# Decoder step: rotary on feature-major heads in place of row-major heads, and a seventh buffer set for expert weights

## The chip, the cores and the metric

The kernel runs on one core of a Trainium2 chip, in float32. The metric is the device time of one launch in microseconds (us), taken as the median of several runs. All other times below are from one profiled execution.

## The reference

One layer of a decoder trunk, for a prompt of 256 tokens and a sample group of 8 tokens (each with 1024 cached positions), 264 tokens in all.

```python
h = rmsnorm(x)
rq, rk, rv, rg, aq, ak, av, gr, ga = split(h @ w_in)        # 8192 columns, 64 groups of 128
rq, aq = rope(rq, pos) * 128**-0.5, rope(aq, pos) * 128**-0.5
rk, ak = rope(rk, pos), rope(ak, pos)                       # x1*cos - x2*sin, x2*cos + x1*sin
r = retention(rq, rk, rv, state)     # 4 heads, chunks of 128; group norm; silu(rg)
a = attention(aq, ak, av, cache)     # 8 heads; the sample group reads 64 cached pages of K and of V
x = x + (sigmoid(gr) * (r @ w_ret_o) + sigmoid(ga) * (a @ w_att_o)) @ w_o
x = x + hier_moe(rmsnorm(x))         # 32 experts (1024 -> 256 -> 1024), two per token
y = rmsnorm(x)                       # outputs: y, the rotated ak, av, the retention states
```

## The kernel before

Every engine runs a program written out by hand, and semaphores tie them together; inside one engine (and inside one DMA-issuing queue) the order is that of the code. A projection unit is 128 output features for all 264 tokens: `features` multiplies 8 weight blocks into `zps[m % 2]` with features on partitions and tokens along the row. Units m = 0 to 63 are the input projection: 0 to 7 the attention queries (one head each), 8 to 15 the keys, 16 to 23 the values, 24 to 27 the retention queries, 28 to 31 the retention keys, 32 to 39 the retention values, 40 to 47 the retention gate, 48 to 63 the two sigmoid gates. Units 64 to 71 multiply by `w_ret_o`, 72 to 79 by `w_att_o`, 80 to 87 by `w_o`. The weights of the units come through a ring of six 1 MB slots (`ring_all`), two units in each.

For m below 40 ScalarE copies `zps` to `zt[m % 2]`, and one unit later TensorE transposes `zt` into rows (three transposes: two blocks of 128 tokens, and 8 sample tokens) in `nps`, which ScalarE copies to `zatt` or `zret` (prompt) and `zdec` or `dret` (sample). GpSimd (`turn`) then rotates the query and key rows in place, two heads at a time with six products or sums: 128x256 each for the prompt, 8x128 each for the sample. TensorE turns rotated heads back to features on partitions where a score needs them: `a_stage(h, 0)` (4 transposes for attention head h, at unit 24 + 3h), `r_stage(r, 0)` (4 for retention head r, at unit 40 + 4r), and `sample_turn` (8 small ones at unit 42). ScalarE copies each result to `qkT`, `rqkT` or `qkd`.

VectorE works at the same time on the sample group's 64 cached key pages (`page`: eight products of 128x128 with a sum, one for each head, L1402). `pages_by(m)` says how many of them stand ahead of unit m in its program: 14 by unit 23, then 7 in four units up to unit 40. Between them stand the softmax steps of the prompt (`a_max` at unit 25 + 3h, `a_scale` after the page behind it), retention (`r_mask`, `r_norm`, `r_gate`) and, from unit 49 on, the sample states. ScalarE waits for `a_max` in its program at unit 25 + 3h, ahead of the `zt` copy of the next unit; TensorE's unit m + 2 waits for that copy. At units 49 to 60 each of the 8 sample states goes through a chain: `gain<-v_rows` from GpSimd's queue, VectorE, TensorE, and out again.

After the projections TensorE multiplies 64 cached value pages (L1087), does `w_ret_o`, `w_att_o` and `w_o`, and the tokens are routed. In the expert stage the tokens of a pair of experts are gathered from `h2_rows` into `xg`, transposed (`x_tr`, L1201), multiplied by gate and up weights (`gate_up`, L1212) and by the down weights, four experts at a time (`quad_down`, L1235). An expert's weights are 3 MB in three 1 MB loads; `SETS` = 6 sets of buffers hold them, placed over buffers that earlier stages no longer need. Loads of experts 0 to 5 stand in SyncE's program ahead of the expert stage; the loads of gate and up of expert e behind them wait for `e_GU` to reach e + 1 - SETS, those of down for `e_D`.

Of the kernel before, what the change touches and what calls it, by code (L numbers as in the profile page):

```python
# [47 lines left out]
SETS = 6  # L48
# [17 lines left out]
def shape_constants():  # L66
# [18 lines left out]
    rope = np.zeros((P, 3, 4, 64), np.float32)  # L85
    for t in range(3):
        pos = i + P * t if t < 2 else np.full(P, PAST, np.float32)
        ang = (pos[:, None].astype(np.float32) * inv[None, :]).astype(np.float32)
        rope[:, t, 0], rope[:, t, 1] = np.cos(ang), np.sin(ang)
        rope[:, t, 2], rope[:, t, 3] = np.cos(ang) * DH ** -0.5, np.sin(ang) * DH ** -0.5  # L90
    put("rope", rope.reshape(P, -1))
# [72 lines left out]
N_ROWS = 40  # L164
# [4 lines left out]
def build(nc, x_prompt, x_sample, cache_k, cache_v, state_ret, page_table, norm_mix, w_in, w_ret_o, w_att_o,  # L169
# [3 lines left out]
    with ctx:  # L173
# [6 lines left out]
        def sem(name):  # L180
# [17 lines left out]
        lgs = sb("lgs", [G + NE, T])  # L198
# [9 lines left out]
        zt = [sb(f"zt{i}", [P, T]) for i in range(2)]  # L208
        qb_all = sb("qb", [P, 2, DM])
# [34 lines left out]

        pw = zr[:, 1984:1984 + NPG * 512 + 64]
# [18 lines left out]
        xgT = [zflat[:, 3 * DM + 512 * i:3 * DM + 512 * (i + 1)] for i in range(2)]  # L264
# [5 lines left out]
        h2n = zflat[:, 0:3 * DM].rearrange("p (t d) -> p t d", t=3)  # L270
# [63 lines left out]
        a_T, a_Tc, a_S, a_P, a_PT, a_PTc, a_O, a_Oc, a_mx, a_ex = map(sem, (  # L334
# [35 lines left out]
        def _(sp):  # L370
# [143 lines left out]
        def _(pool):  # L514
# [114 lines left out]
            for p in range(2):  # L629
                gather_for(p)  # L630
# [1211 lines left out]
```

## Time and profile before

| | |
|---|---|
| median of 3 runs | 761.89 us (760.59 to 765.05) |
| the profiled execution | 762.18 us, of which 760.4 us are the span from first to last instruction |
| busy, share of the span | TensorE 86%, VectorE 40%, ScalarE 19%, GpSimd 18% |
| moved | 243 MB, 320 GB/s over the span |

A busy share is an average over stages with different limits, so the stages are read apart below. The chain of waits is followed back from the last instruction, at each step to what released it; the table of waits says what an engine stood still for. "PEclk" is the clock that was granted to TensorE, as a share of 2.4 GHz.

### The profile page before, as it was taken

To read this page: it belongs to the slowest core of one execution; us is meant where nothing else is said; L and a number is where in the kernel's file an instruction comes from. 1 tells how busy PE (TensorE), PEld (TensorE's weight loads), DVE (VectorE), ACT (ScalarE), POOL (GpSimd) and SP (SyncE) were. 2 spreads that over 40 slices of the span, in tenths; PEclk is the share of its full clock that TensorE was granted. 3 is DMA by queue.
4 is the path that set the end of the run, shared out by engine and by line. 5 is a ranking of instruction groups with operands and counts; after the bars stand their busy time and mean duration, and the time that the engine had idled before them with its cause. 6 is when DMAs were issued, how large, how long until landed. Compare 5 with 4: busy or idle time off the path is not lost.

```text
span 760.4 us, 13782 instructions
## 1 busy us (share of the span) xinstructions
PE 655.6 (86%) x5037; PEld 461.6 (61%) x5037; DVE 306.8 (40%) x1552; ACT 142.4 (19%) x406; POOL 139.0 (18%) x209
## 2 busy tenths in 40 slices
PE   5999999998999978999998999927897879667674
PEld 3888888677888856755432877626653445434331
DVE  3004987998868588610000121354324111111103
ACT  3122223233325322120010000120100101101013
POOL 0169964762000223200000000011000000000000
PEclk9999999999999999999999999957999898899997
DMA  9938989889988988977999989366999999999971
GB/s 309 260 127 281 312 271 401 288 279 342 360 292 281 392 273 287 382 275 275 390 409 386 297 320 409 140 256 239 361 394 401 348 382 401 402 400 402 416 285 59
DMA packets 94918, 243.00 MB, mean 320 GB/s; under 512 B 8850, under 2 KB 54546, under 8 KB 86530
## 3 DMA queue, kind: packets, MB, share of 16 engines
q1 hardware_dynamic: 57906, 192.99, 67.7%
q10 hardware_dynamic: 31328, 32.00, 12.7%
q0 software_dynamic: 5616, 17.11, 6.8%
q8 instruction: 42, 0.69, 0.4%
q14 instruction: 26, 0.21, 0.1%
HBM read 235.00 MB, written 9.11 MB: 321 GB/s over the span
## 4 chain that ended last, share of the span: by engine, by line
PE 56%; DMA 25%; DVE 13%; SPq 2%; issue 2%; ACT 1%; ACTq 0%; POOL 0%; DVEq 0%; POOLq 0%
PE zps L913 32%; DVE kall L1402 6%; PE nps L1087 5%; DMA ring_all<-in_w_up 5%; PE nps L1212 4%; DMA kall<-in_w_up 3%; DMA zret<-in_w_up 3%; DMA gain<-v_rows 3%; DMA qb<-in_w_down 3%; DMA ring_all<-in_w_ret_o 3%; PE zps L1235 3%; DMA out<-sfin 2%; PE nps L884 2%; DMA ring_all<-in_w_down 1%; SPq L444 1%
## 5 line engine op out<-in xcount | busy, mean ns | idle before, releaser
L913 PE MATMUL zps<-hT,ring_all 128*128 128x264 f32 x1152 | 274.8, 393 | 1.6 <-DVE hT L1583 1.0
L913 PEld LDWEIGHTS zps<-hT,ring_all 128*128 128x128 f32 x1152 | 217.4, 193 | 45.0 <-issue 5.3
L1402 DVE CUSTOM_DVE_ANT_0 kall<-kall,qb 128x128 f32<-128x128 f32 x512 | 153.0, 364 | 60.0 <-DMA kall<-in_cache_k 56.9
L620 POOL DMA_INDIRECT zatt<-h_rows,tidx_i x16 | 15.0, 939 | 349.4 <-DVEq L1671 194.4
L913 PE MATMUL zps<-headT,ring_all 128*128 128x264 f32 x256 | 58.5, 388 | 3.7 <-DMA ring_all<-in_w_ret_o 2.3
L913 PEld LDWEIGHTS zps<-headT,ring_all 128*128 128x128 f32 x256 | 48.1, 190 | 14.8 <-issue 4.8
L1087 PE MATMUL nps<-ring_all,zret 128*64 128x512 f32 x224 | 51.6, 599 | 2.8 <-DMA ring_all<-in_cache_v 2.8
L1745 DVE TENSOR_TENSOR qdT<-qdT,nps 128x64 f32<-128x64 f32 x32 | 7.1, 221 | 107.5 <-ACT qdT L825 107.0
L669 ACT ACTIVATE zt<-zps 128x264 f32<-128x264 f32 x56 | 21.8, 390 | 149.4 <-PE zps L913 148.0
L1212 PE MATMUL nps<-ring_all,zatt 128*32 128x128 f32 x768 | 30.0, 311 | 13.9 <-DMA ring_all<-in_w_up 12.4
L1570 DVE TENSOR_TENSOR hT<-zps,zatt 128x264 f32<-128x264 f32 x8 | 3.5, 433 | 93.1 <-PE zps L913 92.9
L1402 DVE DVE_READ_ACCUMULATOR2_ANT scores<- 128x1 f32 x512 | 40.4, 79 | 0.0
L1212 PEld LDWEIGHTS nps<-ring_all,zatt 128*32 128x32 f32 x768 | 25.4, 125 | 17.8 <-issue 16.4
L1761 DVE TENSOR_TENSOR xs<-xs,zps 8x512 f32<-8x512 f32 x15 | 10.1, 675 | 64.3 <-PE zps L1254 64.3
L825 ACT ACTIVATE qdT<-nps 128x64 f32<-128x64 f32 x32 | 7.2, 224 | 144.9 <-PE nps L1212 144.9
L1087 PEld LDWEIGHTS nps<-ring_all,zret 128*64 128x64 f32 x224 | 14.7, 136 | 31.5 <-issue 23.3
L884 PE MATMUL nps<-cst,zt 128*128 128x128 f32 x128 | 22.1, 275 | 3.7 <-ACT zt L669 3.6
L1235 PE MATMUL zps<-zatt,scores 128*32 128x512 f32 x40 | 21.0, 651 | 3.7 <-DMA qb<-in_w_down 3.7
L602 POOL DMA_DIRECT2D gain<-v_rows x16 | 8.8, 549 | 82.7 <-DVE xs L1485 77.7
L1223 PEld LDWEIGHTS nps<-cst,qdT 64*64 64x64 f32 x128 | 6.7, 133 | 28.0 <-issue 27.5
L1235 PE MATMUL zps<-ring_all,scores 128*32 128x512 f32 x88 | 22.4, 630 | 0.7 <-DMA hT<-in_w_down 0.7
L1201 PE MATMUL zps<-cst,zatt 64*128 64x64 f32 x128 | 17.6, 283 | 5.2 <-DMA zatt<-h_rows,tidx_i 5.2
(364 smaller groups left out, 839.5 us busy)
## 6 DMA issues: line engine op xcount, KB each, us to landing
kall<-in_cache_k SPq DMA_DIRECT2D x64, 512.0 KB, 6.4
ring_all<-in_cache_v SPq DMA_DIRECT2D x56, 512.0 KB, 8.2
ring_all<-in_w_in ACTq DMA_DIRECT2D x26, 1024.0 KB, 8.8
ring_all<-in_w_gate SPq DMA_DIRECT2D x12, 1024.0 KB, 15.6
ring_all<-in_w_up SPq DMA_DIRECT2D x12, 1024.0 KB, 17.6
ring_all<-in_w_down SPq DMA_DIRECT2D x10, 1024.0 KB, 15.7
ring_all<-in_w_in SPq DMA_DIRECT2D x6, 1024.0 KB, 13.6
kall<-in_w_gate SPq DMA_DIRECT2D x5, 1024.0 KB, 22.8
```

Of the source, the lines that this page charges most:

```text
L444: sp.dma_start(gate_up_w[b][:, a, :], w[0, bass.ds(e, 1)].rearrange("o (p k) f -> p (o k f)", k=KT)).then_inc(gu_in[b], 16)
L602: pool.dma_start(vb[c], v_rows[b:b + 1, 512 * c:512 * (c + 1)].partition_broadcast(P) .rearrange("p o d -> p (o d)")).then_inc(vb_in[c], 16)
L620: pool.indirect_dma_start(out=rows, out_offset=None, in_=h2_rows, in_offset=bass.IndirectOffsetOnAxis(ap=col, axis=0), bounds_check=T - 1, ...
L669: return act.activation(out, in_, ACT.Copy)
L884: return pe.transpose(out, in_, ident[0:rows, 0:rows])
L913: mm = pe.matmul(zps[m % 2][:, 0:T], w[:, k, P * fb:P * (fb + 1)], rhs[:, k, :], start=(k == 0), stop=(k == KT - 1))
L1087: mm = pe.matmul(nps[0][64 * c:64 * (c + 1), :], pw[:, 512 * p + 64 * b:512 * p + 64 * (b + 1)], pages[:, DM * k + 512 * c:DM * k + 512 * ...
L1201: mm = pe.transpose(zps[0][:, 2 * CAP * k:2 * CAP * k + rows], xg[par][0:rows, k:DM:KT], ident[0:rows, 0:rows])
L1212: mm = pe.matmul(nps[par][CAP * q:CAP * (q + 1), 0:P].rearrange("p (a f) -> p a f", a=2), x[:, 2 * CAP * k:2 * CAP * k + CAP], w[:, :, k, ...
L1235: mm = pe.matmul(bank[CAP * i:CAP * (i + 1), 0:512], acT[q % 2][:, 64 * i + CAP * f:64 * i + CAP * (f + 1)], down_w[b].rearrange("p (f n) ...
L1402: ins = v.tensor_tensor_reduce(kh, kh, qb[b % 2][:, P * h:P * (h + 1)], 1.0, 0.0, ALU.mult, ALU.add, scores[:, pg, AH * b + h:AH * b + h + 1])
L1761: v.tensor_tensor(at, at, bank[0:NB, :], ALU.add).then_inc(e_Sc, 1)
```

## The change

Queries and keys (units 0 to 15 and 24 to 31, `ROTATED`) are rotated as they come out of the projection, with features on partitions. ScalarE makes three copies (`own_copy`): `zps` to `zt`, and its two halves exchanged to `zs`, with the query scale in the copy. GpSimd (`rotate`) multiplies `zt` by cosines, `zs` by signed sines, and adds, each 128x264, into a buffer of the head's own (`turned`). The scores read these buffers, so `a_stage(h, 0)`, `r_stage(r, 0)` and `sample_turn` are gone, with their copies. Rows are made two units after the projection and only for what an output or a row-wise step needs: sample rows alone for attention queries, all for attention keys, none for retention queries, prompt rows for retention keys, which ScalarE scales by the decay on the way to `kdd`. Buffers move to make room: `gain`, `rows_a`, `rows_b` take over work of `zatt` in the expert stage, and `norm_final` is loaded at the end by SyncE. A seventh set of expert weights lies in `zatt` and in `cst`. The gathered rows of odd pairs lie on partitions 64 to 127, and `x_tr` uses a plain product with the identity in place of a transpose.

```diff
-SETS = 6
+SETS = 7
+M_ROWS = 40
+ROTATED = [*range(16), *range(24, 32)]
+ROW_JOBS = [*range(24), *range(28, M_ROWS)]
+def row_jobs(m):
+    return [(j, q) for j, q in enumerate(ROW_JOBS) if q + (2 if q in ROTATED else 1) == m]
...
+            gate_up_in(6, 6)
             sp.wait_ge(z_ready, 2 * (N_IN + 2 * N_O))
             gate_up_in(5, 5)
...
             down_in(1, 1)
+            down_in(6, 6)
...
+            sp.wait_ge(e_GU, NE)
+            sp.dma_start(gain[:, :], norm_final.rearrange("(o d) -> o d", o=1).partition_broadcast(P)
...
-            def turn(x, tmp, tab, rows, nt, q):
-                pool.tensor_tensor(ta, x2, sin, ALU.mult)
-                link(pool.tensor_tensor(tb, x1, sin, ALU.mult))
-                pool.tensor_tensor(x1, x1, cos, ALU.mult)
-                link(pool.tensor_tensor(x2, x2, cos, ALU.mult))
-                pool.tensor_tensor(x1, x1, ta, ALU.subtract)
-                link(pool.tensor_tensor(x2, x2, tb, ALU.add))
+            def rotate(i):
+                m = ROTATED[i]
+                a, _ = COL["rope"]
+                pool.wait_ge(zt_done, m + 1)
+                pool.tensor_tensor(zt[m % 2][:, :], zt[m % 2][:, :], cst[:, a:a + T], ALU.mult)
+                link(pool.tensor_tensor(zs[m % 2], zs[m % 2], cst[:, a + T:a + 2 * T], ALU.mult))
+                pool.tensor_tensor(turned[i], zt[m % 2][:, :], zs[m % 2], ALU.add).then_inc(rope_done, 1)
...
+            def own_copy(m):
+                if m >= 2:
+                    if m - 2 in ROTATED:
+                        act.wait_ge(rope_done, ROTATED.index(m - 2) + 1)
+                    else:
+                        act.wait_ge(n_ready, ROW_JOBS.index(m - 2) + 1)
+                z, ps = zt[m % 2], zps[m % 2]
+                if m in ROTATED:
+                    scale = DH ** -0.5 if m < 8 or 24 <= m < 28 else 1.0
+                    act.activation(z[:, :], ps[:, 0:T], ACT.Copy, scale=scale)
+                    act.activation(zs[m % 2][0:64, :], ps[64:128, 0:T], ACT.Copy, scale=scale)
+                    act.activation(zs[m % 2][64:128, :], ps[0:64, 0:T], ACT.Copy, scale=scale).then_inc(zt_done, 1)
...
-                if k == 0:
-                    pe.wait_ge(rope_done, 8)
-                    for a in range(2):
-                        for t in range(2):
-                            mm = tr(mps[:, 256 * a + P * t:256 * a + P * (t + 1)],
-                                    zatt[:, t, 1024 * a + P * h:1024 * a + P * (h + 1)], P)
-                    mm.then_inc(a_T, 1)
                 if k == 1:
-                    pe.wait_ge(a_Tc, h + 1)
+                    pe.wait_ge(rope_done, 16)
-                    pe.matmul(mps[:, 512:640], qkT[:, 0:128], qkT[:, 256:384], start=True, stop=True)
+                    pe.matmul(mps[:, 512:640], qT[h][:, 0:128], kT[h][:, 0:128], start=True, stop=True)
...
-                    mm = pe.transpose(zps[0][:, 2 * CAP * k:2 * CAP * k + rows], xg[par][0:rows, k:DM:KT], ident[0:rows, 0:rows])
+                    mm = pe.matmul(zps[0][:, 2 * CAP * k:2 * CAP * k + rows], xg[par][0:rows, k:DM:KT], ident[at, at],
+                                   start=True, stop=True, tile_position=(2 * CAP * par, 0))
```

TensorE at units 25 to 27, before (L913 is a projection unit, L884 and L925 make rows or turn heads, L953 and L954 are the scores):

```order
L884 MATMUL nps<-cst,zt 128x128 x2
L925 MATMUL nps<-cst,zt 8x128
L953 MATMUL mps<-scr 128x128
L954 MATMUL mps<-scr 128x256
L913 MATMUL zps<-hT,ring_all 128x264 x8
L884 MATMUL nps<-cst,zt 128x128 x2
L925 MATMUL nps<-cst,zt 8x128
L913 MATMUL zps<-hT,ring_all 128x264 x8
L884 MATMUL nps<-cst,zt 128x128 x2
L925 MATMUL nps<-cst,zt 8x128
L884 MATMUL mps<-cst,sm 128x128 x3
L884 MATMUL mps<-cst,zatt 128x128 x4
```

and in the changed kernel (L903 is the projection unit, L874 a transpose, L952 and L953 the scores):

```order
L903 MATMUL zps<-hT,ring_all 128x264 x8
L952 MATMUL mps<-headT 128x128
L953 MATMUL mps<-headT 128x256
L903 MATMUL zps<-hT,ring_all 128x264 x16
L874 MATMUL mps<-cst,sm 128x128 x3
L903 MATMUL zps<-hT,ring_all 128x264 x8
L952 MATMUL mps<-headT 128x128
L953 MATMUL mps<-headT 128x256
L945 MATMUL mps<-pT,zatt 128x128
L946 MATMUL mps<-pT,zatt 128x128
L947 MATMUL mps<-pT,zatt 128x128
```

The row transposes of the retention queries (`nps<-cst,zt`) and the four transposes of the next head (`mps<-cst,zatt`) are gone from between the units; the scores read `headT`.

GpSimd around the outputs of values, before: two of the output issues, the prompt part of two retention heads, the start of their sample part:

```order
L567 DMA out<-zatt 128x1024 x2
L569 DMA out<-zdec 8x1024
L530 TENSOR_TENSOR rtmp<-zret,cst 128x4x64
L531 TENSOR_TENSOR rtmp<-zret,cst 128x4x64
L532 TENSOR_TENSOR zret<-zret,cst 128x2x2x64
L533 TENSOR_TENSOR zret<-zret,cst 128x2x2x64
L534 TENSOR_TENSOR zret<-zret,rtmp 128x2x2x64
L535 TENSOR_TENSOR zret<-zret,rtmp 128x2x2x64
L530 TENSOR_TENSOR rtmd<-zdec,cst 8x2x64
L531 TENSOR_TENSOR rtmd<-zdec,cst 8x2x64
L532 TENSOR_TENSOR zdec<-zdec,cst 8x2x64
L533 TENSOR_TENSOR zdec<-zdec,cst 8x2x64
```

and in the changed kernel, heads 24 and 25 ahead of all output issues, and head 26 behind them:

```order
L542 TENSOR_TENSOR zt<-zt,cst 128x264
L543 TENSOR_TENSOR zret<-zret,cst 128x264
L544 TENSOR_TENSOR zatt<-zt,zret 128x264
L554 DMA out<-zatt 128x1024 x2
L556 DMA out<-zdec 8x1024
L559 DMA out<-zatt 128x1024 x2
L561 DMA out<-zdec 8x1024
L542 TENSOR_TENSOR zt<-zt,cst 128x264
L543 TENSOR_TENSOR zret<-zret,cst 128x264
L544 TENSOR_TENSOR zatt<-zt,zret 128x264
```

Three 128x264 operations for a head stand where there were six of 128x256 and six of 8x128 for two.

SyncE's queue ahead of the expert stage, before:

```order
L448 DMA ring_all<-in_w_down 128x2x1024 [waits z_ready]
L444 DMA headT<-in_w_gate 128x2048 [waits z_ready]
L444 DMA headT<-in_w_up 128x2048
L444 DMA ring_all<-in_w_gate 128x2048 [waits z_ready]
L444 DMA ring_all<-in_w_up 128x2048
L448 DMA ring_all<-in_w_down 128x2x1024 [waits z_ready]
L448 DMA hT<-in_w_down 128x2x1024 [waits z_ready]
L448 DMA scr<-in_w_down 128x2x1024 [waits logits_T]
L448 DMA qb<-in_w_down 128x2x1024 [waits h2_root]
```

and in the changed kernel:

```order
L456 DMA ring_all<-in_w_down 128x2x1024 [waits z_ready]
L452 DMA zatt<-in_w_gate 128x2048
L452 DMA zatt<-in_w_up 128x2048
L452 DMA headT<-in_w_gate 128x2048 [waits z_ready]
L452 DMA headT<-in_w_up 128x2048
L452 DMA ring_all<-in_w_gate 128x2048 [waits z_ready]
L452 DMA ring_all<-in_w_up 128x2048
L456 DMA ring_all<-in_w_down 128x2x1024 [waits z_ready]
L456 DMA cst<-in_w_down 128x2x1024
L456 DMA hT<-in_w_down 128x2x1024 [waits z_ready]
L456 DMA scr<-in_w_down 128x2x1024 [waits logits_T]
L456 DMA qb<-in_w_down 128x2x1024 [waits h2_root]
```

Gate and up of expert 6 (into `zatt`) now stand ahead of those of expert 5, and its down weights (into `cst`) behind those of expert 1.

## Rows read from the trace of the kernel before

**Rows 1.** The page: TensorE's busy time, and the DMA busy share in 40 slices

```profile
PE 655.6 (86%) x5037; PEld 461.6 (61%) x5037; DVE 306.8 (40%) x1552; ACT 142.4 (19%) x406; POOL 139.0 (18%) x209
...
DMA  9938989889988988977999989366999999999971
```

**Rows 2.** Windows by stage: us, busy us of each engine, PEclk, DMA share, GB/s

```profile
26.50:116.50 90.00, 90.00 (x444) 76.36 (x442) 44.92 (x219) 21.31 (x79) 61.92 (x100) 1.00 0.75 251
116.50:202.90 86.40, 82.39 (x416) 65.35 (x415) 78.00 (x483) 28.22 (x85) 38.55 (x58) 0.98 0.94 334
202.90:248.30 45.40, 45.40 (x244) 39.66 (x243) 35.17 (x256) 19.73 (x46) 1.11 (x2) 1.00 0.84 291
248.30:320.50 72.20, 63.17 (x321) 48.22 (x320) 49.83 (x279) 17.03 (x49) 21.09 (x28) 0.95 0.93 329
320.50:420.00 99.50, 92.91 (x427) 45.02 (x425) 7.62 (x20) 8.26 (x23) 0.00 (x0) 1.00 0.93 349
420.00:492.00 72.00, 70.00 (x321) 55.62 (x320) 15.65 (x45) 4.89 (x12) 0.00 (x0) 1.00 0.78 292
492.00:516.00 24.00, 7.31 (x83) 5.74 (x82) 12.53 (x59) 5.32 (x6) 1.98 (x2) 0.59 0.62 231
516.00:741.00 225.00, 176.60 (x2704) 109.77 (x2704) 48.71 (x158) 25.01 (x87) 13.05 (x14) 0.91 0.97 374
```

**Rows 3.** Chain of waits, 14 to 130 us: start, us, what, count

```profile
26.46 0.33 PE nps L884 x3
...
26.79 3.56 PE zps L913 x16
...
116.26 0.44 PE mps L884 x4
...
120.26 0.22 PE nps L884 x2
...
120.48 0.31 PE nps L925 x2
```

**Rows 4.** TensorE's waits, 14 to 315 us: total, times, longest

```profile
PE nps L1017 <- DVE headT L1468: 4.8, 1, 4.8
...
PE nps L884 <- ACT zt L669: 3.6, 2, 1.9
```

**Rows 5.** Timeline around 130 us: start, us, engine, line, operation

```profile
126.42 0.29 DVE L1402 CUSTOM_DVE_ANT_0 kall<-kall,qb 128x128 f32<-128x128 f32 x1
...
126.54 0.76 POOL L530 TENSOR_TENSOR rtmp<-zret,cst 128x256 f32<-128x256 f32 x1 [7.83 <-ACT zdec L669]
...
126.64 0.81 DVE L1402 CUSTOM_DVE_ANT_0 kall<-kall,qb 128x128 f32<-128x128 f32 x1
...
131.47 0.59 POOL L530 TENSOR_TENSOR rtmd<-zdec,cst 8x128 f32<-8x128 f32 x1
...
134.88 0.28 DVE L1402 CUSTOM_DVE_ANT_0 kall<-kall,qb 128x128 f32<-128x128 f32 x1
```

**Rows 6.** Chain of waits over the whole span

```profile
247.63 17.48 DMA out<-sfin
```

**Rows 7.** Windows ahead of and in the expert stage

```profile
470.00:490.00 20.00, 20.00 (x92) 14.96 (x91) 4.77 (x14) 3.33 (x8) 0.00 (x0) 1.00 0.53 208
505.00:520.00 15.00, 7.54 (x131) 6.22 (x131) 2.70 (x10) 0.03 (x1) 2.91 (x3) 0.50 0.21 67
620.00:680.00 60.00, 45.34 (x649) 27.35 (x638) 9.28 (x20) 6.32 (x22) 3.17 (x4) 0.89 1.02 397
```

**Rows 8.** Timeline of SyncE's queue, first expert load inside the expert stage

```profile
519.97 0.34 SPq L444 DMA_DIRECT2D ring_all<-in_w_gate  x1
```

**Rows 9.** Timeline of TensorE, the first pair's transposes

```profile
514.30 1.11 PE L1201 MATMUL zps<-cst,zatt 64*128 64x64 f32 x8 [5.18 <-DMA zatt<-h_rows,tidx_i]
```

**Rows 10.** Timeline of the tail

```profile
732.43 0.22 ACT L825 ACTIVATE qdT<-nps 128x64 f32<-128x64 f32 x1 [4.28 <-PE nps L1212]
...
748.87 1.21 DVE L1806 TENSOR_TENSOR ring_all<-xs,gain 8x1024 f32<-8x1024 f32 x1 [0.54 <-DVE xs L1761]
```

More of the change, by code:

```diff
@@ L55 @@
 _WIDTHS = [("ident", P), ("ones", P), ("upper", P), ("causal", 3 * P), ("rmask", RH * P), ("rdec", RH * P),
-           ("kdec", RH), ("rope", 3 * 4 * 64), ("edge", EDGES), ("slot", CAP), ("order", NE),
-           ("val", 6), ("tile", XT), ("diag", NB * NB), ("own", AH),
-           ("before", 16), ("after", 16), ("spread", NB * AH)]
+           ("kdec", RH), ("rope", 2 * T), ("diag", NB * NB), ("own", AH), ("spread", NB * AH), ("edge", EDGES), ("slot", CAP),
+           ("order", NE), ("val", 6), ("tile", XT), ("before", 16), ("after", 16)]
 COL, _at = {}, 0
@@ L84, in shape_constants @@
     inv = (np.float32(10000.0) ** (-np.arange(64, dtype=np.float32) / np.float32(64))).astype(np.float32)
[L85 to L91, printed above, removed]
+    pos = np.concatenate([np.arange(S), np.full(NB, PAST)]).astype(np.float32)
+    ang = (pos[None, :] * np.concatenate([inv, inv])[:, None]).astype(np.float32)
+    sign = np.where(i < 64, -1, 1)[:, None]
+    put("rope", np.concatenate([np.cos(ang), sign * np.sin(ang)], 1))
     put("edge", np.tile(CAP * np.arange(1, EDGES + 1) - 0.5, (P, 1)))
@@ L242, in build @@
         vo = zr[:, 0:512]
+        part = lambda ap, at, n: [ap[:, at + T * k:at + T * (k + 1)] for k in range(n)]
+        qT = part(headT[:, 0, :], 0, AH)
+        kT = part(headT[:, 1, :], 0, 5) + part(zflat, 0, 3)
+        rqT = part(scr, 1024, 1) + part(zflat, 3072, 3)
+        rkT = part(zr, 0, 3) + part(zr, 3072, 1)
+        zs = part(zr, 3072 + T, 2)
+        turned = qT + kT + rqT + rkT
         pw = zr[:, 1984:1984 + NPG * 512 + 64]
@@ L263, in build @@
             down_w[i] = ring[(g + 2) % RING]
-        xgT = [zflat[:, 3 * DM + 512 * i:3 * DM + 512 * (i + 1)] for i in range(2)]
+        xgT = [gain[:, 512 * i:512 * (i + 1)] for i in range(2)]
         acT = [scores_f[:, 256 * i:256 * (i + 1)] for i in range(2)]
@@ L622, in gather @@
                                         bounds_check=T - 1, oob_is_err=False).then_inc(x_in2[par], 16)
-            def gather_for(p):
+            for p in range(NPAIR):
                 if p >= 2:
@@ L627, in gather_for @@
                 gather(p % 2, xg[p % 2], tidx_i[0:2 * CAP, p:p + 1])
-            for p in range(2):
-                gather_for(p)
-            for p in range(2, NPAIR):
-                gather_for(p)
             base = link_n[0]
@@ L788, in _ @@
             load_x()
-            act.dma_start(gain[:, :], norm_final.rearrange("(o d) -> o d", o=1).partition_broadcast(P)
-                          .rearrange("p o d -> p (o d)")).then_inc(fgain, 16)
             for k in range(KT):
```

251 lines of the change are left out of this document (105 added, 146 removed).

## Prediction

> **What bounds the kernel now.** I read the page first, then windows by stage, then the chain of waits inside the stages that the change touches. On the page TensorE is busy for 86% of the span and the DMA engines are seldom below 80% [rows 1], so two limits are close everywhere, and the stage decides which one counts. From 26.5 to 116.5 us TensorE never pauses (90.0 of 90.0 us) and the DMA share is 0.75: TensorE is the bound. From 116.5 to 202.9 it is busy for 82.4 of 86.4 us, VectorE for 78.0, and the DMA share is 0.94: three near-bounds. From 202.9 to 248.3 TensorE is full again. From 248.3 to 320.5 it pauses 9 us while the sample states go round. The value stage (320.5 to 420) has 0.93 of DMA beside 92.9 of 99.5 us of TensorE; the next stage is TensorE's, with a DMA share of 0.78; routing (492 to 516) is a chain of small steps, with TensorE at half its clock or little more; and the experts (516 to 741) run at a DMA share of 0.97 with TensorE idle for 48 us: DMA bound [rows 2].
>
> In the chain of waits a projection unit is 3.56 us of products and 0.33 us for three row transposes, 0.11 us each. Turning a head back for the scores is 0.44 us. In the units whose sample rows go to partition 32, rows cost 0.22 us for two transposes and about 0.31 us for the plain product [rows 3]; I round this to 0.63 us a unit for all and 0.31 us for the product.
>
> The 4 us of pauses from 116.5 to 202.9 come from VectorE. In its table of waits 3.6 us, in two pieces, are for ScalarE's `zt` copy [rows 4]; that copy stands behind ScalarE's wait for `a_max`. VectorE is late because of GpSimd. One product of a key page takes 0.29 us alone, and follows the one before by 0.22 us; beside a GpSimd operation it takes 0.81 us. Between 126.64 and 131.47 GpSimd ran six operations of 128x256 and VectorE got eight products through, which alone take 1.7 us of those 4.8: 0.52 us of VectorE lost per operation. From 131.47 to 134.88 six operations of 8x128 let nine products through, 1.9 us of 3.4: 0.25 us lost per operation, however few partitions it has [rows 5].
>
> **The change, part by part.**
>
> Projection, units 2 to 24. Rows of attention queries need one transpose where they needed three: 8 units x 0.22 = 1.8 us. The first head's 0.44 us goes too. TensorE is full here, so all 2.2 us count. ScalarE makes three copies for one, but drops row copies; it is busy for 21 us of these 90 [rows 2], which covers the added 0.3 us each. A new loop appears: the copy of unit m waits for the rotation of m - 2. It costs some 1 us of copies and three GpSimd operations of 0.77 to 0.82 us, 3.5 us in all, against two units of more than 3.6 us each: covered twice. GpSimd alone needs 2.5 us a unit and is covered as well.
>
> Units 25 to 40 (116.5 to 202.9 us). Removed from TensorE: 5 heads x 0.44, retention head 0 at 0.44, the rows of four retention queries at 0.63, and the sample product of four retention keys at 0.31: 6.4 us. The pauses are the second part. From here on VectorE loses to GpSimd, before, 24 operations x 0.52 + 24 x 0.25 + 2.1 us beside two decay products of 128x512 (taken as four of 128x256), 20.6 us; after, 8 heads x 3 x 0.52 = 12.5 us. Its own demand in this stage, 29 key pages x 8 x 0.21 and six softmax steps that I put at 2 us, is 61 us. That makes 82 us before, as much as TensorE was busy, so that each lateness of VectorE became a pause; and 74 us after, beside 82.4 - 6.4 = 76 us of TensorE. With all pauses gone the stage gives 10.4 us. I take 9.5, because the DMA share of 0.94 leaves little: the same 28.9 MB (334 GB/s x 86.4 us) in 76.9 us is 376 GB/s. Bounds: 5.2 us if the DMA time of 0.94 x 86.4 can't be compressed at all, 12 us if the half-clock units after a pause go as well.
>
> The Trainium skill weighs in on both halves of this. "SBUF — State Buffer", section "Who interferes with whom", says that a VectorE operation with two SBUF inputs and a GpSimd operation that reads SBUF exclude each other for a whole instruction. By that as a loss of GpSimd's full 0.8 and 0.55 us the demand before would be 61 + 35 = 96 us, more than the stage took; the trace shows turns being taken, and the loss is the measured 0.52 and 0.25 us. "HBM Reference", section "Specifications (TRN2)", gives 358 GB/s as a core's share of a domain, with more for a core that streams alone; by 358 this stage could not go below 80.7 us and would give 5.7.
>
> Units 41 to 48: two attention heads and two retention heads at 0.44 us and eight transposes of 8 rows (below the 0.9 us of eight full ones; I take 0.6), 2.4 us, of which I count 2.3, TensorE full [rows 2].
>
> Units 49 to 63: the fourth retention head's 0.44 us lies beside pauses of 9 us. One is TensorE's 4.8 us behind VectorE [rows 4], which comes from a 17.5 us write of a 128 KB retention state that `r_norm` waits for [rows 6]. Nothing of that is touched. 0 us; bounds: 5 us either way, since that write may fall into a quieter or a busier moment.
>
> Value stage: 0.5 MB of `norm_final` leaves it, 1.5 us at 349 GB/s [rows 2], half hidden: 0.5 us (0 to 1.5). At the end the same load is issued once the last gate-and-up product is done, 732 us, and is needed at 748.9 us [rows 10]: it costs nothing as long as it lands in 16 us.
>
> Experts. Each load set is 3 MB, 3.15 million bytes, at the 397 GB/s of the steady part [rows 7] 7.9 us. Loads inside the stage start at 520 us [rows 8] and from there DMA bounds it; with seven sets 25 experts are loaded there and not 26. The extra 3 MB needs time ahead of the stage, and there is some: the DMA share is 0.53 from 470 to 490 and 0.21 from 505 to 520 us [rows 7], 21 us idle. Gain 7.9 us; bounds: 0 if the extra loads push experts 5 and 0 to 4 late, 8.4 us at the stage's mean of 374 GB/s.
>
> Its price: `x_tr` becomes eight plain float32 products, each two instructions. The eight transposes take 1.11 us [rows 9]; sixteen instructions at 0.11 to 0.155 us [rows 3] take 1.7 to 2.5 us. The first pair lies on the path to the first `e_GU`, so I add 0.9 us (0 to 1.4). The other 15 lie in TensorE's 48 idle us [rows 2].
>
> Sum: -2.2 - 9.5 - 2.3 - 0.5 - 7.9 + 0.9 = -21.5. The profiled execution took 762.18 us, 0.3 us from the median of the runs, so the sum gives 740.7: **741 us**.
>
> **The rivals.**
>
> A: the front's gain is given back. For it: DMA shares of 0.94 and 0.93 [rows 2], and the sample states' chain, which runs at DMA latency. Against it: TensorE never waits for a projection weight there. If units 25 to 40 give 4 us and the state chain takes 3 us more, the sum is -21.5 + 5.5 + 3 = -13: 749 us.
>
> B: the seventh set gives nothing, because something before 520 us comes late or the queue's `e_D` waits leave gaps. For it: SyncE's queue is in order, and one gap shows in the windows' 0.97. Against it: the same waits come at the same counts. -21.5 + 7.9 = -13.6: 748.5 us.
>
> C: more than forecast: all pauses of units 25 to 40 go and the 17.5 us write with its 4.8 us wait does not recur: -21.5 - 2.5 - 4.8, 733 us.
>
> D: slower: the rotation becomes the pace of 24 units. It decides once a GpSimd operation costs over 1.2 us (3 x 1.2 = 3.6 us, a unit); at 1.6 us it adds 24 x (4.8 - 3.6) = 29 us, and the kernel ends at 741 + 29 = 770 us. Against it: 0.76 us measured for nearly the same shape [rows 5].
>
> **How the numbers follow.** The likeliest case (734 to 747 us by its terms' bounds) has 0.53, A 0.18, B 0.10, C 0.12, D 0.05, and 0.02 is left for something else. A measurement of this kernel tells about 0.5% from no change, 3.8 us. Faster: all but D and a little of A, 0.92; same 0.03; slower 0.05. The range takes in C and A with B: 732 to 753 us.
>
> **What would show it.** In the profile after: the first 24 units in steps of 3.67 us while queries are rotated, and no pauses; units 25 to 40 in 75 to 79 us, with VectorE's mean for L1402's product below 0.33 us from 0.36; GpSimd's three operations at 0.75 to 0.9 us; the stretch of units 49 to 63 still some 70 us; the step from the start of the experts' first product to the last down product about 217 us where it was 225, at 0.97 DMA or more. The prediction is wrong if key pages wait for their DMA for more than 5 us in units 25 to 40 (A), if the expert stage keeps its 225 us (B), or if TensorE waits for ScalarE's copy in units 2 to 24 (D).

## The result, and the profile after

The changed kernel took **768.71 us** in the median of 4 runs (767.35 to 770.15), the kernel before 761.5 us beside it (4 runs): ratio 1.0085, 95% interval 1.0053 to 1.0118. It is slower by 0.9%. I had forecast 741 us, in a range of 732 to 753: the time is outside the range, and the sign is wrong. The profiled execution spans 768.3 us. A run more than 1.5% above the fastest of its kernel is left out of every median and ratio; that is one run in all, in experiment 4.

The page of the changed kernel, first the lines that answer to [rows 1], then two groups of TensorE (matmul and weight load: count | busy us, mean ns | idle before):

```profile
PE 694.2 (90%) x5069; PEld 501.4 (65%) x5069; DVE 282.8 (37%) x1552; ACT 149.0 (19%) x425; POOL 100.9 (13%) x136
...
DMA  9948998899989689879999698837599969999981
...
L1176 PE MATMUL zps<-cst,rows_b 64*128 64x64 f32 x256 | 64.6, 407 | 5.1 <-DMA rows_b<-h_rows,tidx_i 5.1
L1176 PEld LDWEIGHTS zps<-cst,rows_b 64*128 64x128 f32 x256 | 62.1, 331 | 8.5 <-issue 8.5
```

GpSimd and VectorE lost work, as was meant (139.0 to 100.9 us, 306.8 to 282.8). TensorE, which was to lose some 11 us in the front and gain 10 to 22 in the experts, went from 655.6 to 694.2. One line holds it: `x_tr`'s products take 64.6 us.

The windows by stage, cut at the starts of units 25, 41, 49 and 64 and at the experts' first transposition; columns as in [rows 2]. First the kernel after, then the kernel before at the same places:

```profile
113.07:192.92 79.85, 74.94 (x367) 61.64 (x366) 65.78 (x443) 28.48 (x88) 25.52 (x35) 0.96 0.92 326
192.92:230.69 37.77, 37.77 (x192) 32.84 (x191) 32.63 (x237) 13.44 (x31) 1.28 (x3) 1.00 0.91 312
230.69:316.37 85.68, 71.69 (x364) 55.52 (x363) 57.50 (x322) 20.80 (x60) 21.04 (x28) 0.94 0.89 322
505.80:748.90 243.10, 229.99 (x2840) 159.70 (x2840) 49.35 (x158) 24.84 (x87) 13.08 (x14) 0.88 0.87 335
```

```profile
116.53:202.88 86.35, 82.34 (x415) 65.30 (x414) 77.95 (x483) 28.19 (x85) 38.55 (x58) 0.98 0.94 334
202.88:243.19 40.31, 40.31 (x216) 35.14 (x215) 31.16 (x225) 16.65 (x38) 1.11 (x2) 1.00 0.81 278
243.19:324.89 81.70, 72.29 (x368) 55.94 (x366) 57.25 (x320) 21.06 (x60) 21.09 (x28) 0.96 0.94 338
514.30:741.10 226.80, 177.71 (x2712) 110.69 (x2712) 49.19 (x158) 25.01 (x87) 13.05 (x14) 0.90 0.96 371
```

The first column after the window is its length. Units 25 to 40 went from 86.4 to 79.9 us, units 41 to 48 from 40.3 to 37.8, units 49 to 63 from 81.7 to 85.7; the experts' stage from 226.8 to 243.1. It starts 8.5 us earlier than before and ends 7.8 us later. In it TensorE has only 13 idle us of 243, where it had 49 of 227, and the DMA share fell from 0.96 to 0.87. The bound has changed hands: the stage that was the DMA engines' is now TensorE's.

The waits say the same. TensorE's in the expert stage (total us, times, longest), after and then before:

```profile
PE nps L1199 <- DVE qdT L1721: 6.4, 9, 0.8
PE zps L1176 <- DMA rows_b<-h_rows,tidx_i: 5.1, 1, 5.1
PE nps L1211 <- DMA hT<-in_w_down: 3.1, 1, 3.1
PE nps L1188 <- DMA kall<-in_w_up: 1.3, 1, 1.3
```

```profile
PE nps L1212 <- DMA ring_all<-in_w_up: 12.4, 4, 4.3
PE nps L1223 <- DVE qdT L1745: 12.2, 12, 3.4
...
PE nps L1212 <- DMA headT<-in_w_up: 4.9, 2, 4.3
PE nps L1212 <- DMA zdec<-in_w_up: 4.3, 1, 4.3
PE zps L1235 <- DMA qb<-in_w_down: 3.7, 2, 3.2
PE nps L1212 <- DMA kall<-in_w_up: 3.2, 1, 3.2
PE nps L1212 <- DMA zret<-in_w_up: 2.8, 2, 1.7
PE nps L1235 <- DMA ring_all<-in_w_down: 2.2, 1, 2.2
...
PE zps L1235 <- DMA hT<-in_w_down: 0.7, 1, 0.7
```

Before, TensorE waited for expert weights fourteen times, 34.2 us in all; now twice, 4.4 us. The other side of it stands in SyncE's queue, which issues those loads once TensorE has used the buffer: its waits for gate-and-up products grew from 38.1 to 56.7 us, for down products from 76.6 to 99.6.

What one pair costs can be read from TensorE's timeline. After, in the middle of the stage:

```profile
600.79 4.07 PE L1176 MATMUL zps<-cst,rows_b 64*128 64x64 f32 x16
604.78 0.48 PE L1199 MATMUL nps<-cst,qdT 64*64 64x64 f32 x4
605.19 3.64 PE L1188 MATMUL nps<-zatt,gain 128*32 128x128 f32 x64
```

Before, the same three steps:

```profile
519.84 1.09 PE L1201 MATMUL zps<-cst,zatt 64*128 64x64 f32 x8
520.86 0.33 PE L1223 MATMUL nps<-cst,qdT 64*64 64x64 f32 x4
521.12 1.95 PE L1212 MATMUL nps<-ring_all,zatt 128*32 128x128 f32 x64
```

The pair takes 4.07 us where I had put 1.7 to 2.5, and the gate-and-up product right behind it takes 3.64 instead of 1.95 us: it runs at half the clock, and nothing idle stands ahead of it.

### The profile page after: what moved, and what is told of

The parts are those of the page before. It is cut to its first block, busy times and chain, and to the rows that moved or that the text cites. A ratio compares the mean times of both kernels' runs of the same rounds, so it can differ in the third digit from the quotient of the medians.

```text
span 768.3 us, 13775 instructions
## 1 busy us (share of the span) xinstructions
PE 694.2 (90%) x5069; PEld 501.4 (65%) x5069; DVE 282.8 (37%) x1552; ACT 149.0 (19%) x425; POOL 100.9 (13%) x136
## 4 chain that ended last, share of the span: by engine, by line
PE 73%; DMA 15%; DVE 7%; ACT 2%; issue 2%; SPq 1%; ACTq 0%; DVEq 0%; POOLq 0%
PE zps L903 34%; PE nps L1188 8%; PE zps L1176 8%; PE nps L1061 5%; PE zps L1211 4%; DVE kall L1378 3%; DMA kall<-in_w_up 3%; DMA out<-rows_a 3%; DMA ring_all<-in_w_ret_o 3%; DMA gain<-v_rows 2%; PE nps L874 2%; PE bps L1226 2%; DMA hT<-in_w_down 1%; PE zps L874 1%; PE zps L1230 1%
## 5 line engine op out<-in xcount | busy, mean ns | idle before, releaser
L903 PE MATMUL zps<-hT,ring_all 128*128 128x264 f32 x1152 | 273.7, 393 | 1.6 <-DVE hT L1559 1.0
L903 PEld LDWEIGHTS zps<-hT,ring_all 128*128 128x128 f32 x1152 | 217.9, 193 | 45.3 <-issue 4.8
L1378 DVE CUSTOM_DVE_ANT_0 kall<-kall,qb 128x128 f32<-128x128 f32 x512 | 129.0, 317 | 66.1 <-DMA kall<-in_cache_k 63.5
L1176 PE MATMUL zps<-cst,rows_b 64*128 64x64 f32 x256 | 64.6, 407 | 5.1 <-DMA rows_b<-h_rows,tidx_i 5.1
L1176 PEld LDWEIGHTS zps<-cst,rows_b 64*128 64x128 f32 x256 | 62.1, 331 | 8.5 <-issue 8.5
L605 POOL DMA_INDIRECT rows_b<-h_rows,tidx_i x16 | 15.1, 941 | 373.2 <-DMA h_rows<-rows_b 194.6
L903 PE MATMUL zps<-headT,ring_all 128*128 128x264 f32 x256 | 58.5, 388 | 3.7 <-DMA ring_all<-in_w_ret_o 2.3
L903 PEld LDWEIGHTS zps<-headT,ring_all 128*128 128x128 f32 x256 | 48.2, 190 | 14.8 <-issue 4.8
L1714 DVE TENSOR_TENSOR gain<-zps,fT 128x512 f32<-128x512 f32 x16 | 11.1, 691 | 54.2 <-PE zps L1176 54.2
L542 POOL TENSOR_TENSOR zt<-zt,cst 128x264 f32<-128x264 f32 x24 | 18.2, 757 | 88.8 <-ACT zret L696 88.8
L1211 PE MATMUL zps<-ring_all,scores 128*32 128x512 f32 x72 | 27.7, 741 | 0.8 <-DVE xs L1737 0.8
L649 ACT ACTIVATE zt<-zps 128x264 f32<-128x264 f32 x32 | 12.4, 388 | 80.7 <-PE zps L903 78.8
L1188 PE MATMUL nps<-ring_all,gain 128*32 128x128 f32 x640 | 25.1, 313 | 1.0 <-DVE gain L1714 0.9
L1188 PEld LDWEIGHTS nps<-ring_all,gain 128*32 128x32 f32 x640 | 21.0, 127 | 4.5 <-issue 2.4
## 6 DMA issues: line engine op xcount, KB each, us to landing
ring_all<-in_w_up SPq DMA_DIRECT2D x10, 1024.0 KB, 17.7
```

What stands on the lines that cost most here:

```text
L542: pool.tensor_tensor(zt[m % 2][:, :], zt[m % 2][:, :], cst[:, a:a + T], ALU.mult)
L605: pool.indirect_dma_start(out=rows, out_offset=None, in_=h2_rows, in_offset=bass.IndirectOffsetOnAxis(ap=col, axis=0), bounds_check=T - 1, ...
L649: return act.activation(out, in_, ACT.Copy)
L903: mm = pe.matmul(zps[m % 2][:, 0:T], w[:, k, P * fb:P * (fb + 1)], rhs[:, k, :], start=(k == 0), stop=(k == KT - 1))
L1176: mm = pe.matmul(zps[0][:, 2 * CAP * k:2 * CAP * k + rows], xg[par][0:rows, k:DM:KT], ident[at, at], start=True, stop=True, tile_position= ...
L1188: mm = pe.matmul(nps[par][CAP * q:CAP * (q + 1), 0:P].rearrange("p (a f) -> p a f", a=2), x[:, 2 * CAP * k:2 * CAP * k + CAP], w[:, :, k, ...
```

## Experiments

"The transposes" below are the eight `pe.transpose` of a pair, on the rows where the changed kernel keeps them. Ratios are to the kernel before, run beside each; the expert stage is measured from the first pair's transposition to the end of the last wait for down weights. Intervals in brackets are 95% ones.

**1. The product undone in the changed kernel.**

```diff
-                    mm = pe.matmul(zps[0][:, 2 * CAP * k:2 * CAP * k + rows], xg[par][0:rows, k:DM:KT], ident[at, at],
-                                   start=True, stop=True, tile_position=(2 * CAP * par, 0))
+                    mm = pe.transpose(zps[0][:, 2 * CAP * k:2 * CAP * k + rows], xg[par][0:rows, k:DM:KT], ident[at, at])
```

> The changed kernel with x_tr's eight transposes back in place of the plain float32 products with the identity (odd pairs still on partitions 64 to 127). Theory 1 (the sixteen product instructions, 4.0 us a pair where eight transposes took 1.1, make TensorE the bound of the expert stage): the pairs take 1.1 us again, the stage is DMA bound with 25 experts to load, about 219 us from the first pair's transposes to the last down weights where the changed kernel has 243 and the kernel before 227; 743 to 747 us in all. Theory 2 (the seventh set spoils the order of loads in SyncE's queue, and the products only fill time that is waited anyway): 760 us or more. Theory 3 (most of the loss is TensorE's half clock after slow loads of weights, and stays with transposes): 750 to 758 us.

Measured: 746.35 us (743.44 to 747.67), ratio 0.9768 [0.9705, 0.9831]. Its stage, and its page's groups of the same line:

```profile
504.20:726.60 222.40, 176.54 (x2712) 112.27 (x2712) 49.20 (x158) 25.02 (x87) 13.02 (x14) 0.90 0.96 366
```

```profile
L1176 PE MATMUL zps<-cst,rows_b 64*128 64x64 f32 x128 | 17.7, 286 | 5.2 <-DMA rows_b<-h_rows,tidx_i 5.2
L1176 PEld LDWEIGHTS zps<-cst,rows_b 64*128 64x128 f32 x128 | 15.4, 199 | 9.1 <-issue 9.0
```

The DMA share is back at 0.96, and all else that the change does is worth 2.3%. The product costs 1.0085 - 0.9768 = 0.032 of the kernel's time, 24 us.

**2. The product alone, in the kernel before** (the same edit the other way round, in its `x_tr`).

> The kernel before with one edit: x_tr makes plain float32 products with the identity in place of transposes, all pairs on partitions 0 to 63. Theory 1: the stage was DMA bound with 48 us of TensorE idle, and 16 x 2.9 = 46 us of work plus slower clocks eat that up, so it gets 12 to 25 us slower: 774 to 787 us. Theory 2 (the products are hidden by DMA, the set order is the cause): 762 to 765 us.

Measured: 785.26 us (783.26 to 788.6), ratio 1.0287 [1.0218, 1.0356]; stage 251.2 us, TensorE busy for 235.45 of them, where before it had 177.71 of 226.8. The cost is there without rotation, without the seventh set, and with rows in other buffers.

**3 and 4. Six sets in the changed kernel, with the product and with the transposes.** `SETS = 6`, without the seventh's buffers and its two loads.

```diff
-SETS = 7
+SETS = 6
-            gate_up_in(6, 6)
-            down_in(6, 6)
```

> The changed kernel with six sets of expert weights: the loads of expert 6 ahead of the stage are gone, all else as changed. Theory 1 (TensorE bound in the expert stage): the set is worth little there, 0 to 5 us slower than the changed kernel, 768 to 774 us. Theory 2 (the seventh set is the cause of the loss): 15 us or more faster than the changed kernel, 754 us or less.

> The changed kernel with transposes in x_tr and six sets: what the rotation on features and the moved buffers give alone. By the windows of the two traces the front is 8.5 us ahead when the experts start, so theory 1 expects 752 to 754 us, and the difference to the run with seven sets and transposes is the worth of the set, 7.9 us by the load rate. If the set is worth nothing (rival B of the prediction), both are at 753 us.

Measured: with the product 780.51 us (778.04 to 781.9), ratio 1.0216 [1.0151, 1.028], and a stage of 254 us, which is more than either theory said (0 to 5 us over the changed kernel, or 15 us under it); with transposes 755.45 us (750.22 to 760.09 in nine runs; a tenth took 762.19), ratio 0.9888 [0.9851, 0.9925]:

```profile
506.90:737.80 230.90, 180.41 (x2712) 112.74 (x2712) 49.28 (x158) 24.95 (x87) 13.03 (x14) 0.89 0.96 367
```

So three parts stand side by side. Rotation and rows: 0.9888, -8.5 us. The seventh set: 0.9888 to 0.9768, -9.1 us by the times (with the two intervals, some 3.5 to 14.6) and 8.5 us by the stage (230.9 to 222.4). The product: +24 us. The set helps beside the product too (1.0216 to 1.0085, 10 us, where I expected 0 to 5), although TensorE has only 13 to 17 idle us in those two stages; so loads still count where TensorE is nearly full.

One thing does not fit. Experiment 4 has six sets and transposes, as the kernel before, and its stage takes 230.9 us where that one's took 226.8. Its profiled run took 760.09 us, 4.6 us more than its median, so the stage may be long by chance; against the kernel before, seven sets make it only 4.4 us shorter (222.4). Which of the two is the set's worth inside the stage, single traces don't tell.

**5. Is it the number of instructions, or what they read?** The product's weights were every eighth column of the rows, `k:DM:KT`. Here they are 128 neighbouring columns, so the experts get their input features in another order; the number and the shape of all instructions and loads stay the same.

```diff
-xg[par][0:rows, k:DM:KT]
+xg[par][0:rows, P * k:P * (k + 1)]
```

> The price of x_tr's product by itself: the changed kernel, but the stationary operand is a contiguous block of 128 columns of the gathered rows in place of every eighth column, so the experts get their input features in another order than their weights. Same instructions, same counts. Theory 1a (the strided read of the float32 stationary operand is what costs 0.25 us an instruction, its weight load 0.33 us): sixteen instructions take about 1.8 us a pair (0.11 us each) and the kernel takes 745 to 750 us. Theory 1b (it is the plain float32 product of 64 rows, however its operand lies): 4 us a pair again, 768 us.

One run: 755.13 us, span 753.3, stage 229.1.

```profile
L1176 PE MATMUL zps<-cst,rows_b 64*128 64x64 f32 x256 | 33.6, 284 | 4.8 <-DMA rows_b<-h_rows,tidx_i 4.8
L1176 PEld LDWEIGHTS zps<-cst,rows_b 64*128 64x128 f32 x256 | 31.3, 196 | 8.0 <-issue 8.0
```

The instructions are as many, and of the same shape. One weight load takes 0.196 us, not 0.331. A pair takes 2.00 us at full clock, inside the 1.7 to 2.5 that my term assumed. The transposes read every eighth column too and load in 0.199 us. So it is neither the count nor the stride alone: plain float32 weights with a stride of 32 bytes are the slow ones. What stands behind a pair tells of the clock (windows of this kernel on a pair and on the gate-and-up product after it, then the same two of the changed kernel):

```profile
612.00:614.00 2.00, 2.00 (x19) 1.93 (x20) 0.22 (x1) 0.22 (x1) 0.00 (x0) 1.00 1.01 414
614.19:615.96 1.77, 1.77 (x68) 1.77 (x68) 0.54 (x1) 0.22 (x1) 0.94 (x1) 1.00 1.03 419
```

```profile
600.79:604.86 4.07, 4.07 (x19) 3.95 (x20) 0.22 (x1) 0.22 (x1) 0.00 (x0) 0.83 1.02 407
605.19:608.60 3.41, 3.41 (x66) 3.15 (x68) 0.39 (x1) 0.22 (x1) 0.93 (x1) 0.50 1.05 428
```

The granted clock (the number behind POOL's) falls during the slow pair and stands at 0.50, 1.2 GHz, behind it, with TensorE listed as busy throughout.

Is the pair slow because the clock is low, or because DMA traffic disturbs the reads? Two other pairs of the changed kernel answer, the first at clock 0.50 and one at clock 1.00, both with the DMA engines almost silent:

```profile
505.77:509.80 4.03, 4.03 (x16) 3.85 (x16) 0.00 (x0) 0.00 (x0) 0.00 (x0) 0.50 0.05 18
550.20:554.20 4.00, 4.00 (x24) 3.93 (x24) 0.22 (x1) 0.22 (x1) 0.00 (x0) 1.00 0.01 4
```

The strided pair takes 4.0 us at either clock, with or without DMA traffic. The contiguous pair does depend on the clock: 2.00 us at 1.00, and 3.64 us for the first pair of the stage, at 0.50.

**6 and 7. The front's remaining waits.** Two buffers, with a semaphore each, for the outgoing retention state; and key pages planned further ahead (20 by unit 24, 22 more by unit 40, where it was 14 and 28). Both with the transposes.

```diff
-        s1, sfin = rows_a[:, 512:768], rows_a[:, 768:1024]
+        s1, sfins = rows_a[:, 512:768], [rows_a[:, 768:1024], rows_a[:, 256:512]]
...
-                if r >= 1:
-                    v.wait_ge(r_st, 16 * r)
+                if r >= 2:
+                    v.wait_ge(r_sts[r % 2], 16 * (r // 2))
```

```diff
     if m < 24:
-        return m - 9
+        return 20 * (m - 9) // 14
     if m < 40:
-        return 14 + 7 * (m - 23) // 4
+        return 20 + 22 * (m - 23) // 16
```

> The changed kernel with transposes in x_tr and two buffers (with a semaphore each) for the retention state on its way out, so that r_norm of head r waits for the write of head r - 2. Theory (the wait of the prediction's stretch of units 49 to 63: VectorE stands 5.4 us for one write and TensorE 5.8 us behind it): the stretch gets 3 to 6 us shorter, 738 to 743 us. Rival (the sample states' chain of transfers sets that stretch anyway): same as with one buffer, 744 to 747 us.

> The changed kernel with transposes in x_tr and the key pages spread anew: 20 of them ahead of unit 24 in place of 14, 22 in place of 28 in units 24 to 40. VectorE stood 12.6 us for the first score there, while TensorE later stood 4.5 us for it. Theory (units 25 to 40 are bound by VectorE's lateness beside GpSimd's rotations): the pause goes and the stage is 3 to 5 us shorter, 740 to 744 us. Rival (page loads bound it: VectorE waited in 14 places for them): same, 744 to 748 us.

Measured: two buffers 742.83 us (740.54 to 744.67), ratio 0.9758 [0.9724, 0.9791]; pages ahead 742.78 us (740.3 to 745.39), ratio 0.9752 [0.9715, 0.9789]. Both medians are in the range of the theory that was expected (738 to 743 and 740 to 744), but against the kernel before beside them neither is told apart from experiment 1. TensorE's waits from 14 to 320 us, of the two in this order:

```profile
PE mps L877 <- DVEq L1398: 4.4, 1, 4.4
PE nps L994 <- DVE headT L1446: 1.4, 1, 1.4
```

```profile
PE nps L991 <- DVE headT L1443: 9.5, 1, 9.5
...
PE mps L874 <- DVEq L1395: 1.1, 3, 0.6
```

Each takes away its own wait and leaves the other: with two buffers the wait for the state's write is 1.4 us (5.8 in experiment 1), with pages ahead the pause behind VectorE is 1.1 us (4.5 in experiment 1), but the write takes 21.8 us here and is waited for 9.5 us. That need not be the pages' doing: this write and this wait differ as much between kernels with the same code up to there (see units 49 to 63 below).

**8. Both edits.**

> Both of the edits before this one on the changed kernel with transposes. If both theories hold the gains add: 735 to 740 us. If the sample states' chain takes over, 740 to 744 us.

Measured: **736.8 us** (735.83 to 741.42), ratio 0.9679 [0.9641, 0.9716]: the fastest of all, 3.2% under the kernel before and 4.0% under the changed one (0.9679 against 1.0085). Against its two neighbours, run on the same chip, it is 6 us better: here the two edits together show what neither did alone. Both waits are gone:

```profile
PE mps L877 <- DVEq L1398: 0.9, 1, 0.9
...
PE nps L994 <- DVE headT L1446: 0.6, 1, 0.6
```

The waits for the sample states grew beside them, 8.2 us in five where experiment 1 had 4.2 in three, so that chain has taken over part of the gain.

**9 to 11. What does a microsecond of TensorE cost in the expert stage?** My prediction let 15 of 16 pairs lie in TensorE's idle time ("covered" in what follows). Three doses of added work test that: products for the eight even pairs only, each transpose issued twice, and experiment 5's form again, timed.

```diff
+                    if par == 0:
+                        mm = pe.matmul(..., xg[par][0:rows, k:DM:KT], ident[at, at], ...)
+                    else:
+                        mm = pe.transpose(..., xg[par][0:rows, k:DM:KT], ident[at, at])
```

```diff
+                    for again in range(2):
+                        mm = pe.transpose(..., xg[par][0:rows, k:DM:KT], ident[at, at])
```

> The changed kernel with transposes for the eight odd pairs and the float32 products, every eighth column of the rows as their weights, for the eight even ones. It tells what a microsecond of TensorE's work costs in the expert stage. The products cost 2.94 us more than the transposes a pair (4.03 against 1.09), 23.5 us for eight. Theory shared: loads are released by TensorE's products and TensorE waits for the loads, so a fixed part of each added microsecond is passed on; from all sixteen pairs, 20.7 us more stage (243.1 against 222.4) for 46.9 us more product time (64.6 against 17.7), 0.44. Then the stage takes 222.4 + 10.4 = 232.8 us and the kernel 746.35 + 10.4 = 756.7 us, ratio 0.990 to before. Theory covered, on which my prediction rested: idle TensorE microseconds take up the work until they are used up, and only the rest counts. Then the first 26 us cost nothing but the first pair's 2.9 us: stage 225 to 226 us, kernel 749 us, ratio 0.981.

> The changed kernel with transposes in place of the products, each of the eight transposes of a pair issued twice into the same place. The instructions are the cheap ones and TensorE has as many as with the products, 16 a pair, some 2.1 us against 1.09: 16 us more work in all. Theory shared: 0.44 of it is passed on, 7 us; stage 229.5 us, kernel 753.5 us, ratio 0.986, as for the products on contiguous columns. Theory covered: only the first pair's 1 us counts, stage 223.5 us, kernel 747.5 us, ratio 0.978.

> The float32 products with a contiguous block of 128 columns of the rows as their weights, as in the single look at this form, now timed. The experts get their input features in another order, so the outputs are of other numbers; the amount of work and of loads is the same. Theory shared: 2.00 us a pair against 1.09, 14.6 to 15.9 us more TensorE time, 6.4 to 7 us more stage than with transposes: 229 us, kernel 753 us, ratio 0.986. Theory covered: stage 223.5 us, kernel 747.5 us, ratio 0.978, and the single look's 229.1 us would be chance.

Measured: even pairs 756.92 us (752.54 to 763.75, 10 runs), ratio 0.9914 [0.9876, 0.9953]; twice 751.39 us (747.69 to 756.6), ratio 0.9836 [0.9778, 0.9893]; contiguous 753.65 us (750.39 to 761.2), ratio 0.9878 [0.9815, 0.9941]. The groups of `x_tr` in these three, in this order:

```profile
L1177 PE MATMUL zps<-cst,rows_b 64*128 64x64 f32 x128 | 32.4, 419 | 4.8 <-DMA rows_b<-h_rows,tidx_i 4.8
L1180 PE MATMUL zps<-cst,rows_b 64*128 64x64 f32 x64 | 8.8, 277 | 0.0
```

```profile
L1177 PE MATMUL zps<-cst,rows_b 64*128 64x64 f32 x256 | 31.7, 282 | 5.1 <-DMA rows_b<-h_rows,tidx_i 5.1
```

```profile
L1176 PE MATMUL zps<-cst,rows_b 64*128 64x64 f32 x256 | 35.7, 295 | 5.4 <-DMA rows_b<-h_rows,tidx_i 5.4
```

Worked out from these groups and the stages, over the 17.7 us and 222.4 us of experiment 1:

| kernel | added in `x_tr` | stage | longer by | passed on |
|---|---|---|---|---|
| transposes twice | 14.0 us | 225.4 | 2.9 | 0.2 |
| contiguous (5) | 15.9 | 229.2 | 6.8 | 0.4 |
| contiguous, again | 18.0 | 229.5 | 7.0 | 0.4 |
| even pairs | 23.5 | 231.0 | 8.5 | 0.4 |
| changed kernel | 46.9 | 243.2 | 20.8 | 0.4 |

"Covered" wanted 1 us for the second and third row and 2.9 for the fourth, and ratios of 0.978 and 0.981; the intervals of contiguous and of even pairs leave these out. These expectations priced the first pair too low: it runs at half clock, and from its start to the second pair's start contiguous products take 2.3 to 2.5 us more than transposes, not 1. That makes the contiguous case weaker evidence, but some 4.5 us of its stage remain over it; the even pairs, 11 us slower than experiment 1 by the ratios with less than 3 us for the first pair, decide against "covered" by themselves. "Shared", a fixed 0.44, comes within 2 us of the stage in those three; for the doubled transposes it wanted 7 us and ratio 0.986, and the stage gave 2.9 us, at a ratio whose interval holds both theories' values. That stage began 3.5 us later than experiment 1's (507.75 against 504.23 us), with as much more time for loads ahead of it, and by the ratios the run is 5 us slower, not 2.9. So idle time in a stage that loads bound does not swallow added work whole; whether the share passed on is a constant these runs don't tell.

## Why the prediction was wrong

Point by point, in its own order.

*Units 2 to 24, -2.2 us.* Unit 25 began 3.5 us earlier than before, at 113.07 and not 116.53 us; 0.4 us of it was already there at the start of the first stage. The 3.1 us left are 0.9 more than forecast, and the right kind: one transpose where there were three. The rotation was hidden as forecast: GpSimd's operations take 0.74 to 0.89 us, the units keep steps of 3.67 us (28.69, 32.36, 36.03), and rival D's mechanism does not occur, though its number, 770 us, is the one that came true. A rival's time can be hit for a reason that it didn't name.

*Units 25 to 40, -9.5 us (5.2 to 12).* -6.5 us: within the bounds, mis-sized. VectorE's product does get cheaper, 0.341 us in the mean of these units against 0.372 (0.317 against 0.364 over the whole span), less than the 0.33 that I had named as the sign. And one pause of 4.8 us remained (141.88 us), where TensorE waits for VectorE's softmax. VectorE was late there because it had stood still before: its program holds too few pages ahead of the first score (14 by unit 23), and it finished them and waited for TensorE's product:

```profile
DVE sm L1386 <- PE mps L953: 12.8, 1, 12.8
```

Experiment 7 puts six more pages ahead of unit 24: VectorE's wait goes to 0.3 us and TensorE's pause to 1.1. My sum of VectorE's demand counted only its work inside the stage and not that it could use the time ahead of it. The sign for rival A did come up, key pages that wait for their DMA for more than 5 us (7.5 us in seven waits, 3.7 before), but it isn't what makes the pause: in experiment 7 these waits are 9.2 us and the pause is gone. Nor was my doubt about 376 GB/s tested: the stage moved only 326 GB/s, since more was loaded ahead of it (286 GB/s in the first stage, 251 before).

*Units 41 to 48, -2.3 us.* -2.5 us. Right.

*Units 49 to 63, 0 (-5 to 5).* +4.0 us. The chain of waits has the retention state's write at 21.4 us, where [rows 6] had 17.5, and TensorE's wait behind it grew from 4.8 [rows 4] to 9.1 us:

```profile
235.13 21.43 DMA out<-rows_a
```

```profile
PE nps L991 <- DVE headT L1444: 9.1, 1, 9.1
```

That is rival A's kind of loss, but its size is in part chance. The changed kernel and experiments 1, 5, 9, 10 and 11 have the same code up to here, and in them the write takes 16.3 to 21.4 us and the wait is 4.0 to 9.1 us; the kernel before and experiment 2 have 17.5 and 18.2 us, and 4.8 and 5.5. Over all eleven kernels with one buffer the write is 16.3 to 22.2 us long, so such a width belongs in the range. Two buffers end the wait (experiment 6). (My "some 70 us" for these units came from the window 248.30 to 320.50 [rows 2], which is not cut at their starts; so cut they took 81.7 us before.)

*Value stage, -0.5 us.* 0: the lead over the kernel before is 8.5 us at unit 64 and 8.5 us at the first pair.

*Experts, -7.9 us for the set.* Right by the times, -9.1, with the wide interval above. By the stage it is -8.5 or -4.4, depending on which six-set trace is taken; the 217 us that I had named came out at 222.4 with transposes.

*The price of `x_tr`, +0.9 us (0 to 1.4).* This is **the step that failed**, and it alone turned the sign: +24 us by the times of experiment 1, and +22 us in the kernel before (experiment 2, ratio 1.0287). Two of its sentences were wrong. "Sixteen instructions at 0.11 to 0.155 us": the 0.11 came from transposes and the 0.155 from a plain product whose weights are eight neighbouring columns [rows 3], both at full clock, and these read every eighth column of float32; 4.03 us a pair. At half clock, which [rows 7] shows for the time of the first pair, even contiguous products take 3.64 us, 2.5 more than the transposes, so the bound of 1.4 us was too low for the first pair alone. And "the other 15 lie in TensorE's 48 idle us": even at 2.00 us a pair, inside my bounds, 7 us of 16 to 18 come out at the end. At 4.03 us the stage's idle time is spent (13 us left of 49), and TensorE is its bound.

The Trainium skill had a rule for the first of the two, and I did not use it. "SBUF — State Buffer", in the note on cachelines in its section "Door 1: The DMA port swizzle", says that reads are fast while they stay in a 16-byte line, so that four float32 is as far as one can stride for free. The columns here are eight apart. The products agree with it, 0.331 against 0.196 us a load; the transposes do not, with 0.199 us at the same stride.

With this one term at its measured 24 us, and the rest as forecast, the sum would have been 741 - 0.9 + 24 = 764 us; the 4.6 us that are missing are units 25 to 40 and 49 to 63 (3.0 and 4.0 us short) and the value stage (0.5) against a better set and first stage. My "734 to 747 us by its terms' bounds" was too narrow as well: the bounds add up to 731 to 759 us.

**To carry on.** A duration read from a trace belongs to its operand's layout too: before a plain product takes the place of a transpose, compare the stride of what becomes the weights, and if no row has it, let the upper bound say so. And idle time of an engine inside a stage bound by loads is not free room when that engine's own products release the load buffers; price added work there at up to half of its length, and look at which engine is next to full. A wait that comes from when a DMA falls (here a 128 KB write beside 1 MB loads) differs from run to run even where no edit stands ahead of it (4.0 to 9.1 us here); give it a width, or a second buffer.

## What the runs showed of the hardware that I had not expected

A float32 weight load of 64x128 takes 0.196 us from neighbouring columns and 0.331 us from every eighth column in a plain product, but 0.199 us from every eighth column in a transpose. Sixteen of the slow loads take 4.0 us at granted clock 0.50 and at 1.00 alike. In the pair at 600.79 us, 4.07 us in which the profile lists TensorE as busy without a gap, the granted clock goes from 1.00 to 0.50, and the gate-and-up product behind takes 3.64 us. That does not follow every such pair: in experiment 2 the product behind the pair at 643.46 us runs at 1.00 and takes 1.95 us. Behind 2.00 us of contiguous products (experiment 5, at 612.00 us), or behind 1.09 us of transposes (experiment 1, at 580.56 us), it stays at 1.00, and the gate-and-up product takes 1.95 or 1.96 us; the first of these:

```profile
614.19 1.95 PE L1188 MATMUL nps<-zdec,gain 128*32 128x128 f32 x64
```

How much of the 24 us is this half clock was not measured by itself. By an estimate it is the smaller part: TensorE's busy time in the stage rose by 53.5 us over experiment 1 (229.99 against 176.54), of which `x_tr` is 46.9 us, and `x_tr` itself costs the same at either clock. The Trainium skill's "TensorE: Matmul & The Clock Gate", Part 4, says that the full clock does not engage for transposes; here the products behind them run at full clock, so no run of this case shows a loss from it.
